# A new order of work at the entry and the segment turns of a feed-forward block

## The chip, the cores and the metric

The kernel runs on one core of one Trainium2 chip: TensorE (matmuls), VectorE, ScalarE, GpSimd and SyncE (DMA queues), each with its own instruction stream, tied together by semaphores. The metric is device time in microseconds (us), lower is better.

## The reference

One layer of a hybrid encoder over two sequences (1024 and 512 tokens of 1024 features, with 16 meta tokens in front): a norm, one input projection, two kinds of windowed attention, a norm for each, an output projection, and then the feed-forward part, which is where the change lies:

```
mix = jnp.concatenate([_rmsnorm(oa, outn_a_g), _rmsnorm(ob, outn_b_g)], axis=-1)
x = x + mix @ w_out
h = _rmsnorm(x, norm2_g)
x = x + (jax.nn.silu(h @ w_gate) * (h @ w_up)) @ w_down
```

The hidden width is 2816; all values are 32-bit floats.

## The kernel before

Products are made in near 32-bit precision from three matmuls: each operand is split in a high and a low part, and `product()` (L396 to L398) adds high x high, low x high and high x low. ScalarE writes high parts (`sth`, `mvh`, `acth`, `dh`), VectorE and GpSimd subtract them to get low parts (`stl`, `mvl`, `actl`, `dl`).

The feed-forward part goes over three segments of 512 tokens. Each segment has 11 cycles (`PASS`), one for 256 hidden columns; `cycles` (L690) writes the first two and the last of a segment out (q = 0, 1, 10) and loops over the rest (q is None). The 33 cycles c run through without a gap. In a cycle TensorE makes the gate of its columns, then the up part, then `down` of the cycle before, 8 blocks of 6 matmuls (a tile of 128 tokens t, half of the 1024 columns each). Gate and up are 2 x 2 block products in a scheme of seven products in place of eight, 12 matmuls each: seven standing operands (weights or sums of them: `weight_sums`, four a matrix, L1992 to L1998) against seven moving ones (tokens or sums of them: `token_sum`, L2013, eight instructions a segment). Products are combined by VectorE: `first_sums` (`u`, L2024, L2027) make room in PSUM for products 6 and 7, `last_sum` (L2033) gives the result. ScalarE makes silu, VectorE multiplies (`times`, L2043), splits (`act_low`, L2047), and adds what `down` gives to y (`add_down`, L2055). `down` waits before its third block, and at each later one, for an add two blocks ago.

The moving parts of the next segment are made in the last cycle of a segment, the turn (c = 10 and 21): seven `mvh` on ScalarE, seven `mvl` on VectorE (L2017). The entry is cycle 0 with what leads to it: the last output projection tiles are added to y (`mix_adds`, L1963), normed (`normed2`, `xn`, L1941), transposed by TensorE (`turn2`, L2417) and copied out by ScalarE (`mix_out`, `qm`, L1536), while the gate of segment 0 begins. Tiles (5,0) and (5,1) are the last two, and belong to segment 2.

Nothing plans the order: the order of the code is the order of each engine's queue, and an engine stands still at the first instruction that waits. GpSimd makes `stl` 0, 3, 4, 5 and 6 (L1195) and the two `dl` (L1201); VectorE makes `stl` 1 and 2 (L2002). SyncE loads the weights of `down` (`draw`) once `turn2` is through. Some buffers share memory: `xn[0]` with the end of `stl`, `xn[1]` with the first `draw`, `junk2` with the first `dl`.

Of the kernel before, what the change touches and what calls it, by code (L numbers as in the profile page):

```python
# [12 lines left out]
P = 128  # L13
# [51 lines left out]
def hybrid_encoder_layer(nc, x_prompt, x_sample, meta_tokens, t5_table, norm1_g, w_in, qn_a_g, kn_a_g,  # L65
# [134 lines left out]
    g2 = s("g2", [P, D])  # L200
    junk2 = s("junk2", [P, D])
    osq = s("osq", [P, KT, P])
    osum = [s(f"osum{i}", [P, 2, P]) for i in range(2)]
# [27 lines left out]

    tsum = [[at(f"tsum0{i}", [P, 4, 2 * P], F32, a) for i, a in enumerate((dl1_at, t_at, t_at + 4096, t_at + 8192))]]
    tsum += [[at(f"tsum1{i}", [P, 4, 2 * P], F32, qm_at[0] + i * 4096) for i in range(4)]] * 2
# [10 lines left out]
    with ExitStack() as ctx:  # L244
# [806 lines left out]
        def _(pool):  # L1051
# [160 lines left out]
            for i in ST_POOL:  # L1212
                if i == 5:
                    pool.wait_ge(turned2, 22)
                standing_low(0, graw, i)
# [5 lines left out]
        def _(act):  # L1221
# [349 lines left out]

            def standing_high(n, raw, i):
                if i in S_NEEDED:
                    act.wait_ge(s_done, n * 4 + S_NEEDED[i])
                wait(act, prod, n * 7 + i - 6)
                act.activation(sth[:, i, :, :], standing(raw, i), ACT.Copy).then_inc(st_hi, 1)  # L1576
# [35 lines left out]
            def ffn_cycle(c, g, q):  # L1612
                gate_n, up_n = c * 2, c * 2 + 1
                last = q == PASS - 1 and g == NSEG - 1

                def up_high(i):
                    standing_high(up_n, uraw, i)
# [12 lines left out]
                for i in range(3):  # L1630
                    up_high(i)
                wait(act, act_lo, c * 2)
                silu((0, 0), X, prod, gate_n * 7 + 4)
                for i in range(3, 7):
                    up_high(i)
                for i, at_ in enumerate(ORDER):
                    silu(at_, hidden(*at_), comb, gate_n * 5 + 3 + i)
                if last:
                    down_high(c)
                else:  # L1640
                    block21(c * 2 + 2, graw, gate_in, c + 1)
                first_product(up_n)
                for i in range(7):
                    gate_high(i)
                if q == 0 and g == 0:
                    mix_out(5, 1)

# [3 lines left out]
            act.wait_ge(mix_mm, 24)  # L1651
            for i in range(7):
                moving_high(0, i)
                standing_high(0, graw, i)
                if i == 0:
                    mix_out(4, 1)
                elif i == 2:
                    act.wait_ge(y_spilled[2], 32)
                    first_product(0)
                elif i == 3:  # L1660
                    block21(1, uraw, up_in, 0)
            mix_ss(5, 1)
            mix_out(5, 0)
            act.activation(ssq[:, 0:1], eps[:, :], ACT.Silu)
# [5 lines left out]
        def _(dve):  # L1670
# [261 lines left out]

            def normed2(i, slot, first):
# [5 lines left out]
                if not first:  # L1939
                    dve.wait_ge(turned2, tile_ * 2 - 2)  # L1940
                dve.scalar_tensor_tensor(out=xn[slot][:, :],  # L1941
                                         in0=y[:, bass.ds(tile_, 1), :].rearrange("p o c -> p (o c)"),
                                         scalar=r_, in1=g2[:, :], op0=ALU.mult, op1=ALU.mult).then_inc(xn2_done, 1)
# [43 lines left out]

            def weight_sums(n, raw):

                a = quarters(raw)  # L1990
                dve.wait_ge(a21_out, n + 1)
                dve.tensor_tensor(S1, A21_OR_S2, a[1, 1], ALU.add).then_inc(s_done, 1)  # L1992
                dve.tensor_tensor(a[1, 0], a[0, 0], A21_OR_S2, ALU.subtract).then_inc(s_done, 1)
                dve.wait_ge(s_done, n * 4 + 2)
                dve.tensor_tensor(A21_OR_S2, S1, a[0, 0], ALU.subtract).then_inc(s_done, 1)
                wait(dve, st_lo_pool, n * 5)
                dve.wait_ge(s_done, n * 4 + 3)
                dve.tensor_tensor(sum4[:, :, :], a[0, 1], A21_OR_S2, ALU.subtract).then_inc(s_done, 1)  # L1998

            def standing_low(n, raw, i):  # L2000
# [58 lines left out]
            def ffn_cycle(c, g, q):  # L2059
# [8 lines left out]

                if q == 0 and g == 1:
                    dve.wait_ge(turned2_out, 24)  # L2070

                def tokens_sum(n):
                    if q in (0, 1) and g < NSEG - 1 and n < 4:
                        token_sum(g + 1, 4 * q + n)

                tiles = down_tiles(g, q)
                if not first:
                    act_low(c - 1, 0)
                    act_low(c - 1, 1)
                weight_sums(up_n, uraw)  # L2080
                if not first:
                    first_sums(gate_n)
                standing_low(up_n, uraw, 1)
                standing_low(up_n, uraw, 2)
                for i in range(3):
                    last_sum(gate_n, i, hidden(*ORDER[i]))
                if first:
                    normed2(5, 1, False)
                    dve.wait_ge(turned2_out, 16)
                    for n in range(4):  # L2090
                        tokens_sum(n)
                else:
                    for t in tiles[0]:
                        add_down(c - 1, g, q, t, tokens_sum)
# [6 lines left out]
                if not last:  # L2101
                    standing_low(c * 2 + 2, graw, 2)
                times(c, up_n, -1)
                for i in range(3):
                    last_sum(up_n, i, (Y, Z, W)[i])
                    times(c, up_n, i)
                    if i < 2:
                        tokens_low(1 + i)
                tokens_low(3)
                if not first:  # L2110
                    for t in tiles[1]:
                        add_down(c - 1, g, q, t, tokens_sum)
                        if t < 3:
                            tokens_low(4 + t)

            group_sums(5, 0)
            group_inverses(5, 0)
            for half in range(2):
# [4 lines left out]
            dve.wait_ge(turned2_out, 8)  # L2123
            dve.wait_ge(y_spilled[1], 32)
            for n in range(4):
                token_sum(0, n)
            group_inverses(5, 1)
            mix_adds(5, 1, 0)
            weight_sums(0, graw)
            normed2(5, 0, False)  # L2130
            token_sum(0, 4)
            token_sum(0, 5)
            mix_adds(5, 1, 1)
            moving_low(0, 0)
            standing_low(0, graw, 1)
            moving_low(0, 1)
            standing_low(0, graw, 2)
            moving_low(0, 2)
            dve.wait_ge(y_spilled[2], 32)
            token_sum(0, 6)  # L2140
            token_sum(0, 7)
            moving_low(0, 3)
            first_sums(0)
            for i in range(4, 7):
                moving_low(0, i)
# [8 lines left out]
        def _(pe):  # L2154
# [253 lines left out]

            def turn2(i, slot, first=False):

                pe.wait_ge(xn2_done, i * 2 + slot + 1)
                for b in range(2):
                    if not first:
                        pe.wait_ge(turned2_out, i * 4 + slot * 2 + b - 1)
                    for k in range(4):
                        c = (4 * b + k) * P
                        op = pe.transpose(bank[4 + b][:, k * P:(k + 1) * P], xn[slot][:, c:c + P], ident[:, :])  # L2417
                    op.then_inc(turned2, 1)
# [9 lines left out]
            def seven_products(n, c, g, q, gate):  # L2428
                for i in range(7):
                    if i == 0 and gate and q == 0 and g == 0:  # L2430
                        pe.wait_ge(mix_add, 24)
                    if i == 2 and gate and q == 0 and g == 0:
                        turn2(5, 0)
                    if gate and q == 0:
# [34 lines left out]
            def ffn_cycle(c, g, q):  # L2469
# [75 lines left out]
```

## Time and profile before

| | us |
|---|---|
| median of 3 runs | 1969.75 |
| lowest, highest | 1966.92, 1971.46 |
| profiled execution | 1972.3 |
| its span | 1970.5 |
| TensorE busy | 1860.9 (94%) |
| VectorE busy | 1301.2 (66%) |
| ScalarE busy | 1003.8 (51%) |
| GpSimd busy | 959.2 (49%) |

The span is the time from the first to the last instruction; what is missing to the execution's own time (1.8 us) lies around it. TensorE's mean granted clock is 0.977. Over the whole kernel TensorE stands first on the chain that ended last (56%), VectorE follows with 5%. The feed-forward part begins at about 900 us.

### The profile page before, as it was taken

How to read it: one execution, taken by the hardware profiler on the slowest of the kernel's cores; microseconds unless marked ns; L12 is line 12 of the kernel's file. 1: busy time of each engine (PE TensorE's matmuls, PEld its weight loads, DVE VectorE, ACT ScalarE, POOL GpSimd, SP SyncE). 2: the span in 40 equal slices, each digit the busy share in tenths (PEclk: the TensorE clock that was granted, in tenths of full speed). 3: DMA queues.
4: the chain of work that ended last, by engine and by line, in shares of the span. 5: the costliest groups of instructions: out<-in, count | busy, mean ns of one | idle time of the engine just before them, and what ended most of it. 6: DMA issues, size and time to landing. Idle time of an engine off the chain costs nothing.

```text
span 1970.5 us, 35333 instructions
## 1 busy us (share of the span) xinstructions
PE 1860.9 (94%) x12047; PEld 1670.4 (85%) x12047; DVE 1301.2 (66%) x2345; ACT 1003.8 (51%) x2085; POOL 959.2 (49%) x811
## 2 busy tenths in 40 slices
PE   5998898999898989997999999999999999999998
PEld 4797677999677877886899999899999989999997
DVE  2656657888566876548666666776666676666664
ACT  3555456888535883345444354544444354444432
POOL 1334235765335651114556464646556464645543
PEclk7999998999998998999999999999999999999999
DMA  5443632454322435011332332343332335323221
GB/s 155 131 144 113 169 98 72 112 150 135 97 86 84 148 114 202 32 63 56 120 116 86 105 106 85 108 171 108 103 109 89 103 101 178 107 86 123 89 85 65
DMA packets 184323, 217.10 MB, mean 110 GB/s; under 512 B 13124, under 2 KB 162100, under 8 KB 183964
## 3 DMA queue, kind: packets, MB, share of 16 engines
q1 hardware_dynamic: 184220, 215.77, 34.9%
q8 instruction: 60, 0.98, 0.2%
q14 instruction: 43, 0.35, 0.1%
HBM read 197.34 MB, written 27.27 MB: 114 GB/s over the span
## 4 chain that ended last, share of the span: by engine, by line
PE 56%; DVE 5%; ACT 2%; issue 2%; POOL 1%; DMA 0%; ACTq 0%; POOLq 0%; DVEq 0%; SPq 0%
PE bank L396 19%; PE bank L397 18%; PE bank L398 18%; DVE mvl L2017 1%; POOL msl L1124 1%; ACT msh L1501 0%; DVE qm L1914 0%; ACT logit L1407 0%; DVE tsum L2013 0%; ACT qm L1431 0%; DVE pmeta L1854 0%; DVE logit L1839 0%; PE bank L2305 0%; DVE ptl L1846 0%; PE bank L2283 0%
## 5 line engine op out<-in xcount | busy, mean ns | idle before, releaser
L396 PE MATMUL bank<-mvh,sth 128*128 128x256 f32 x1848 | 526.4, 285 | 17.6 <-DVE act_f L2033 5.6
L398 PE MATMUL bank<-mvh,stl 128*128 128x256 f32 x1848 | 525.3, 284 | 0.0
L397 PE MATMUL bank<-mvl,sth 128*128 128x256 f32 x1848 | 525.3, 284 | 0.0
L396 PEld LDWEIGHTS bank<-mvh,sth 128*128 128x128 f32 x1848 | 356.8, 193 | 20.9 <-issue 16.9
L397 PEld LDWEIGHTS bank<-mvl,sth 128*128 128x128 f32 x1848 | 357.0, 193 | 1.2
L398 PEld LDWEIGHTS bank<-mvh,stl 128*128 128x128 f32 x1848 | 356.9, 193 | 0.0
L1201 POOL TENSOR_TENSOR dl<-draw,dh 128x1024 fp32r<-128x1024 f32 x66 | 157.9, 2414 | 365.9 <-ACT dh L1594 365.9
L2055 DVE TENSOR_TENSOR y<-bank,y 128x512 f32<-128x512 f32 x264 | 182.4, 691 | 163.9 <-PE bank L398 163.0
L1056 POOL TENSOR_TENSOR wl<-wraw,wh 128x1024 fp32r<-128x1024 f32 x54 | 130.5, 2418 | 263.5 <-ACT wh L1252 263.5
L1195 POOL TENSOR_TENSOR stl<-graw,sth 128x512 fp32r<-128x512 f32 x132 | 178.2, 1350 | 101.6 <-ACT sth L1576 97.4
L396 PE MATMUL bank<-dh,acth 128*128 128x512 f32 x528 | 209.5, 397 | 7.7 <-DVE y L2055 5.3
L396 PE MATMUL bank<-hth,wh 128*128 128x512 f32 (+2 forms) x512 | 198.1, 387 | 12.1 <-DVE htl L1764 8.6
L397 PE MATMUL bank<-dl,acth 128*128 128x512 f32 x528 | 208.4, 395 | 0.0
L398 PE MATMUL bank<-dh,actl 128*128 128x512 f32 x528 | 207.9, 394 | 0.0
L1610 ACT ACTIVATE acth<-act_f 128x512 fp32r<-128x512 f32 x66 | 38.2, 624 | 322.3 <-PE bank L398 314.3
L398 PE MATMUL bank<-hth,wl 128*128 128x512 f32 (+2 forms) x512 | 187.5, 366 | 0.0
L397 PE MATMUL bank<-htl,wh 128*128 128x512 f32 (+2 forms) x512 | 186.6, 364 | 0.0
L1195 POOL TENSOR_TENSOR stl<-uraw,sth 128x512 fp32r<-128x512 f32 x132 | 169.6, 1309 | 4.6 <-ACT sth L1576 4.6
L1730 DVE RECIPROCAL rt_p<-rt_p 128x512 f32<-128x512 f32 (+2 forms) x30 | 84.4, 2826 | 79.0 <-ACT rt_p L1321 79.0
L1407 ACT ACTIVATE logit<-logit,negm 128x274 f32<-128x274 f32 (+1 forms) x192 | 113.8, 593 | 38.9 <-DVE negm L1839 37.8
L396 PEld LDWEIGHTS bank<-hth,wh 128*128 128x128 f32 x512 | 98.3, 192 | 38.1 <-POOL wl L1056 12.9
L396 PEld LDWEIGHTS bank<-dh,acth 128*128 128x128 f32 x528 | 99.7, 189 | 30.9 <-DVE y L2055 6.5
(248 smaller groups left out, 4257.6 us busy)
## 6 DMA issues: line engine op xcount, KB each, us to landing
graw<-in_w_gate SPq DMA_DIRECT2D x33, 1024.0 KB, 5.4
uraw<-in_w_up SPq DMA_DIRECT2D x33, 1024.0 KB, 5.4
draw<-in_w_down SPq DMA_DIRECT2D x66, 512.0 KB, 4.1
wraw<-in_w_in SPq DMA_DIRECT2D x54, 512.0 KB, 3.9
bias_rows<-table_a SPq DMA_DIRECT2D x36, 192.0 KB, 3.1
out<-y SPq DMA_DIRECT2D x12, 512.0 KB, 3.0
bias<-table_b SPq DMA_DIRECT2D x28, 201.0 KB, 2.6
table_a<-line_a_dram SPq DMA_DIRECT2D x8, 576.0 KB
```

Source lines behind the costliest of these rows:

```text
L396: pe.matmul(out, lhs[0], rhs[0], start=start, stop=False, skip_group_check=True)
L397: pe.matmul(out, lhs[0], rhs[1], start=False, stop=False, skip_group_check=True)
L398: return pe.matmul(out, lhs[1], rhs[0], start=False, stop=stop, skip_group_check=True)
L1056: pool.tensor_tensor(wl[G % 2][:, :, :], wraw[G % 2][:, :, :], f32(wh[G % 2][:, :, :]), ALU.subtract).then_inc(w_lo, 1)
L1124: pool.tensor_tensor(msl[slot][:, :, :], mix_tile(i, slot), f32(msh[slot][:, :, :]), ALU.subtract).then_inc(ms_lo, 1)
L1195: pool.tensor_tensor(stl[:, i, :, :], standing(raw, i), f32(sth[:, i, :, :]), ALU.subtract).then_inc(st_lo_pool, 1)
L1201: pool.tensor_tensor(dl[j][:, :], draw[j][:, :], f32(dh[j][:, :]), ALU.subtract).then_inc(down_lo, 1)
L1407: act.activation(x, x, ACT.Exp, bias=negm[:, h % 2, t:t + 1], scale=-1.0, accum_out=lsum[:, h % 2, t:t + 1]).then_inc(expd, 1)
L1610: act.activation(acth[:, j, :], act_f[:, j, :], ACT.Copy).then_inc(act_hi, 1)
L1730: op = dve.reciprocal(rt[:, u0:u0 + w], rt[:, u0:u0 + w])
L2017: dve.tensor_tensor(mvl[:, i, :, :], moving(g, i), f32(mvh[:, i, :, :]), ALU.subtract).then_inc(mv_lo, 1)
L2055: dve.tensor_tensor(yt, DOWN_BANK[half][:, :], yt, ALU.add).then_inc(y_add, 1)
```

## The change

The arithmetic is the same; instructions change places, and two buffers. On VectorE at the turn, `mvl` 2 to 6 of the next segment go behind the pairs of adds of `down`. At the entry, `xn` of tiles (5,0) and (5,1) go to the end of cycle 0 and get buffers of their own (`last_xn`); the first `mvl` goes ahead of the last `mix_adds`; three of the four weight sums of the first up matrix go between `mvl` 4 and 5 and the fourth behind the last sums of the gate. Token sums of the next segment are all made in the segment's second cycle instead of four in the first and four in the second; those of segment 0 go earlier. TensorE makes `turn2(5,0)` before the last up product of cycle 0 instead of before the third gate product. ScalarE's silu and copies of those tiles follow. GpSimd's and SyncE's orders don't change.

```diff
-    tsum = [... (dl1_at, t_at, t_at + 4096, t_at + 8192) ...]
+    last_xn = [xn[1], junk2]
+    tsum = [... (t_at, t_at + 4096, dl1_at, t_at + 8192) ...]
...
             for i in ST_POOL:
                 if i == 5:
-                    pool.wait_ge(turned2, 22)
+                    pool.wait_ge(turned2, 18)
...
+                if q == 0 and g == 0:
+                    up_high(0)
+                    silu((0, 0), X, prod, gate_n * 7 + 4)
+                    up_high(1)
+                    up_high(2)
...
                 for i in range(7):
                     gate_high(i)
-                if q == 0 and g == 0:
-                    mix_out(5, 1)
+                    if q == 0 and g == 0 and i >= 5:
+                        mix_out(5, i - 5)
...
             for i in range(7):
+                if i == 0:
+                    standing_high(0, graw, 0)
+                    moving_high(0, 0)
+                    mix_out(4, 1)
+                    continue
                 moving_high(0, i)
                 standing_high(0, graw, i)
...
+                elif i == 4:
+                    mix_ss(5, 1)
-            mix_ss(5, 1)
-            mix_out(5, 0)
...
+            def fourth_sum(n, raw):
+                a = quarters(raw)
                 wait(dve, st_lo_pool, n * 5)
                 dve.wait_ge(s_done, n * 4 + 3)
                 dve.tensor_tensor(sum4[:, :, :], a[0, 1], A21_OR_S2, ALU.subtract).then_inc(s_done, 1)
...
                 def tokens_sum(n):
-                    if q in (0, 1) and g < NSEG - 1 and n < 4:
-                        token_sum(g + 1, 4 * q + n)
+                    if q == 1 and g < NSEG - 1:
+                        token_sum(g + 1, n)
...
-                weight_sums(up_n, uraw)
                 if not first:
+                    weight_sums(up_n, uraw)
                     first_sums(gate_n)
                 standing_low(up_n, uraw, 1)
-                standing_low(up_n, uraw, 2)
+                if not first:
+                    standing_low(up_n, uraw, 2)
                 for i in range(3):
                     last_sum(gate_n, i, hidden(*ORDER[i]))
+                    if first and i == 1:
+                        standing_low(up_n, uraw, 2)
                 if first:
-                    normed2(5, 1, False)
-                    dve.wait_ge(turned2_out, 16)
-                    for n in range(4):
-                        tokens_sum(n)
+                    fourth_sum(up_n, uraw)
...
+                if first:
+                    for slot in range(2):
+                        normed2(5, slot, False, True)
                 times(c, up_n, -1)
                 for i in range(3):
                     last_sum(up_n, i, (Y, Z, W)[i])
                     times(c, up_n, i)
-                    if i < 2:
-                        tokens_low(1 + i)
-                tokens_low(3)
+                    if i == 0:
+                        tokens_low(1)
                 if not first:
                     for t in tiles[1]:
                         add_down(c - 1, g, q, t, tokens_sum)
-                        if t < 3:
-                            tokens_low(4 + t)
+                        tokens_low(2 + t)
+                    if turn:
+                        tokens_low(6)
...
             weight_sums(0, graw)
-            normed2(5, 0, False)
-            token_sum(0, 4)
-            token_sum(0, 5)
+            moving_low(0, 0)
             mix_adds(5, 1, 1)
-            moving_low(0, 0)
...
             moving_low(0, 2)
+            moving_low(0, 3)
             dve.wait_ge(y_spilled[2], 32)
             token_sum(0, 6)
             token_sum(0, 7)
-            moving_low(0, 3)
             first_sums(0)
-            for i in range(4, 7):
+            moving_low(0, 4)
+            bank_sums(1, uraw)
+            for i in range(5, 7):
                 moving_low(0, i)
...
                 for i in range(7):
-                    if i == 0 and gate and q == 0 and g == 0:
-                        pe.wait_ge(mix_add, 24)
-                    if i == 2 and gate and q == 0 and g == 0:
-                        turn2(5, 0)
+                    if i in (0, 2) and gate and q == 0 and g == 0:
+                        pe.wait_ge(mix_add, 23 + i // 2)
+                    if i == 6 and not gate and q == 0 and g == 0:
+                        turn2(5, 0, last=True)
...
                 if first:
-                    turn2(5, 1)
+                    turn2(5, 1, last=True)
                     pe.wait_ge(turned2_out, 24)
```

VectorE at the entry before, from the second `u` of gate 0 (it ends in PSUM as `u_156`; `uraw` is the up weights, `sum_149` the fourth weight sum):

```order
L2027 TENSOR_TENSOR u_156<-bank,u_155 128x256 [waits comb,prod]
L2017 TENSOR_TENSOR mvl<-tsum_161,mvh 128x1024 [waits mv_hi]
L2017 TENSOR_TENSOR mvl<-qm,mvh 128x1024 [waits mv_hi]
L2017 TENSOR_TENSOR mvl<-tsum_162,mvh 128x1024 [waits mv_hi]
L1992 TENSOR_TENSOR bank<-bank,uraw 128x512 [waits a21_out]
L1993 TENSOR_TENSOR uraw<-uraw,bank 128x4x128
L1995 TENSOR_TENSOR bank<-bank,uraw 128x512 [waits s_done]
L1998 TENSOR_TENSOR sum_149<-uraw,bank 128x512 [waits s_done,st_lo_pool]
L2002 TENSOR_TENSOR stl<-bank,sth 128x512 [waits st_hi] x2
L2033 TENSOR_TENSOR act_f<-bank,u_156 128x256 [waits comb,prod] x2
```

The same place after:

```order
L2047 TENSOR_TENSOR u_156<-bank,u_155 128x256 [waits comb,prod]
L2037 TENSOR_TENSOR mvl<-tsum_161,mvh 128x1024 [waits mv_hi]
L2004 TENSOR_TENSOR bank<-bank,uraw 128x512 [waits a21_out]
L2005 TENSOR_TENSOR uraw<-uraw,bank 128x4x128
L2007 TENSOR_TENSOR bank<-bank,uraw 128x512 [waits s_done]
L2037 TENSOR_TENSOR mvl<-qm,mvh 128x1024 [waits mv_hi]
L2037 TENSOR_TENSOR mvl<-tsum_162,mvh 128x1024 [waits mv_hi]
L2022 TENSOR_TENSOR stl<-bank,sth 128x512 [waits st_hi]
L2053 TENSOR_TENSOR act_f<-bank,u_156 128x256 [waits comb,prod] x2
L2022 TENSOR_TENSOR stl<-bank,sth 128x512 [waits st_hi]
L2053 TENSOR_TENSOR act_f<-bank,u_155 128x256 [waits comb,prod]
L2014 TENSOR_TENSOR sum_149<-uraw,bank 128x512 [waits s_done,st_lo_pool]
```

Three of the weight sums stand between two `mvl` now, one `stl` and the fourth sum behind last sums (`act_f`), and `xn` is gone from here.

VectorE at the first turn before, from the fourth `mvl` on (`tsum_16x` and `qm` are the next segment's tokens and their sums, `y` the adds of `down`):

```order
L2017 TENSOR_TENSOR mvl<-qm,mvh 128x1024 [waits mv_hi]
L2055 TENSOR_TENSOR y<-bank,y 128x512 [waits down_mm] x2
L2017 TENSOR_TENSOR mvl<-tsum_165,mvh 128x1024 [waits mv_hi]
L2055 TENSOR_TENSOR y<-bank,y 128x512 [waits down_mm] x2
L2017 TENSOR_TENSOR mvl<-qm,mvh 128x1024 [waits mv_hi]
L2055 TENSOR_TENSOR y<-bank,y 128x512 [waits down_mm] x2
L2017 TENSOR_TENSOR mvl<-tsum_166,mvh 128x1024 [waits mv_hi]
L2055 TENSOR_TENSOR y<-bank,y 128x512 [waits down_mm] x2
L2047 TENSOR_TENSOR actl<-act_f,acth 128x512 [waits act_hi,turned2_out]
L2047 TENSOR_TENSOR actl<-act_f,acth 128x512 [waits act_hi]
```

The same place after, from the first add on:

```order
L2075 TENSOR_TENSOR y<-bank,y 128x512 [waits down_mm] x2
L2037 TENSOR_TENSOR mvl<-tsum_163,mvh 128x1024 [waits mv_hi]
L2075 TENSOR_TENSOR y<-bank,y 128x512 [waits down_mm] x2
L2037 TENSOR_TENSOR mvl<-qm,mvh 128x1024 [waits mv_hi]
L2075 TENSOR_TENSOR y<-bank,y 128x512 [waits down_mm] x2
L2037 TENSOR_TENSOR mvl<-tsum_165,mvh 128x1024 [waits mv_hi]
L2075 TENSOR_TENSOR y<-bank,y 128x512 [waits down_mm] x2
L2037 TENSOR_TENSOR mvl<-qm,mvh 128x1024 [waits mv_hi]
L2037 TENSOR_TENSOR mvl<-tsum_166,mvh 128x1024 [waits mv_hi]
L2067 TENSOR_TENSOR actl<-act_f,acth 128x512 [waits act_hi] x2
```

An `mvl` stands behind each pair of adds, two behind the last, and then the two `actl`.

## Rows read from the trace of the kernel before

**Rows 1.** Windows; busy us of each engine, granted PE clock, DMA share, GB/s.

```profile
900.00:950.00 50.00, 35.68 (x240) 34.37 (x241) 38.43 (x54) 29.31 (x53) 27.86 (x17) 0.87 0.30 95
1000.00:1200.00 200.00, 200.00 (x1375) 186.07 (x1375) 130.24 (x231) 88.06 (x165) 108.79 (x74) 1.00 0.30 98
```

**Rows 2.** Timeline, ScalarE's `acth`, one pair a cycle; start, us, what, idle before.

```profile
1225.25 1.15 ACT L1610 ACTIVATE acth<-act_f 128x512 fp32r<-128x512 f32 x2 [10.01 <-PE bank L398]
...
1261.26 1.15 ACT L1610 ACTIVATE acth<-act_f 128x512 fp32r<-128x512 f32 x2 [11.69 <-PE bank L398]
...
1292.54 1.15 ACT L1610 ACTIVATE acth<-act_f 128x512 fp32r<-128x512 f32 x2 [10.01 <-PE bank L398]
...
1574.06 1.15 ACT L1610 ACTIVATE acth<-act_f 128x512 fp32r<-128x512 f32 x2 [10.01 <-PE bank L398]
...
1608.77 1.16 ACT L1610 ACTIVATE acth<-act_f 128x512 fp32r<-128x512 f32 x2 [10.39 <-PE bank L398]
```

**Rows 3.** Timeline, TensorE, down blocks in both turns.

```profile
1245.72 0.39 PE L396 MATMUL bank<-dh,acth 128*128 128x512 f32 x1
...
1251.31 0.80 PE L396 MATMUL bank<-dh,acth 128*128 128x512 f32 x1 [2.66 <-DVE y L2055]
...
1254.04 0.46 PE L396 MATMUL bank<-dh,acth 128*128 128x512 f32 x1
...
1258.27 0.40 PE L396 MATMUL bank<-dh,acth 128*128 128x512 f32 x1
...
1600.10 0.50 PE L396 MATMUL bank<-dh,acth 128*128 128x512 f32 x1 [2.64 <-DVE y L2055]
```

**Rows 4.** Timeline, VectorE, first turn.

```profile
1250.58 1.27 DVE L2055 TENSOR_TENSOR y<-bank,y 128x512 f32<-128x512 f32 x2
...
1262.00 1.29 DVE L2047 TENSOR_TENSOR actl<-act_f,acth 128x512 fp32r<-128x512 f32 x2
...
1266.45 0.42 DVE L2027 TENSOR_TENSOR u<-bank,u 128x256 f32<-128x256 f32 x1
```

**Rows 5.** Timeline, TensorE, entry of the feed-forward part.

```profile
901.45 0.35 PE L396 MATMUL bank<-mvh,sth 128*128 128x256 f32 x1 [4.15 <-DVE mvl L2017]
...
920.26 0.55 PE L396 MATMUL bank<-mvh,sth 128*128 128x256 f32 x1 [5.63 <-DVE act_f L2033]
...
933.72 0.55 PE L396 MATMUL bank<-mvh,sth 128*128 128x256 f32 x1 [3.36 <-DVE u L2027]
...
939.84 0.39 PE L396 MATMUL bank<-mvh,sth 128*128 128x256 f32 x1 [0.82 <-ACT qm L1536]
```

**Rows 6.** Timeline, GpSimd, after the first turn.

```profile
1263.44 4.78 POOL L1201 TENSOR_TENSOR dl<-draw,dh 128x1024 fp32r<-128x1024 f32 x2 [11.66 <-ACT dh L1594]
```

**Rows 7.** Timeline, VectorE, entry, beside GpSimd's `stl`.

```profile
905.94 1.22 DVE L2017 TENSOR_TENSOR mvl<-qm,mvh 128x1024 fp32r<-128x1024 f32 x1
...
910.58 2.31 DVE L2017 TENSOR_TENSOR mvl<-qm,mvh 128x1024 fp32r<-128x1024 f32 x1
...
924.93 3.48 DVE L2013 TENSOR_TENSOR tsum<-qm 128x512 f32<-128x512 f32 x2
```

**Rows 8.** Timeline, GpSimd, the same stretch.

```profile
905.45 2.86 POOL L1195 TENSOR_TENSOR stl<-graw,sth 128x512 fp32r<-128x512 f32 x1 [5.55 <-ACT sth L1576]
...
911.76 2.27 POOL L1195 TENSOR_TENSOR stl<-graw,sth 128x512 fp32r<-128x512 f32 x1
...
926.14 1.73 POOL L1195 TENSOR_TENSOR stl<-graw,sth 128x512 fp32r<-128x512 f32 x1
```

**Rows 9.** Timeline, VectorE, a steady cycle.

```profile
982.29 0.42 DVE L2033 TENSOR_TENSOR act_f<-bank,u 128x256 f32<-128x256 f32 x1 [0.55 <-PE bank L398]
```

**Rows 10.** Timeline, VectorE, entry, before `mvl` and before the last sums.

```profile
897.48 1.29 DVE L2013 TENSOR_TENSOR tsum<-qm 128x512 f32<-128x512 f32 x2
...
918.50 1.29 DVE L2002 TENSOR_TENSOR stl<-bank,sth 128x512 fp32r<-128x512 f32 x2 [0.67 <-ACT sth L1576]
```

**Rows 11.** Timeline, ScalarE, entry.

```profile
896.46 1.06 ACT L1582 ACTIVATE mvh<-qm 128x1024 fp32r<-128x1024 f32 x1 [3.29 <-PE bank L398]
```

More of the change, by code:

```diff
@@ L229, in hybrid_encoder_layer @@
     assert BASE + s.offset <= END
-    tsum = [[at(f"tsum0{i}", [P, 4, 2 * P], F32, a) for i, a in enumerate((dl1_at, t_at, t_at + 4096, t_at + 8192))]]
+    tsum = [[at(f"tsum0{i}", [P, 4, 2 * P], F32, a) for i, a in enumerate((t_at, t_at + 4096, dl1_at, t_at + 8192))]]
     tsum += [[at(f"tsum1{i}", [P, 4, 2 * P], F32, qm_at[0] + i * 4096) for i in range(4)]] * 2
@@ L1569, in _, with standing_high @@
             group_root(5, 1)
-            def standing_high(n, raw, i):
+            def standing_high(n, raw, i, after_banks=False):
                 if i in S_NEEDED:
-                    act.wait_ge(s_done, n * 4 + S_NEEDED[i])
+                    act.wait_ge(s_done, n * 4 + (3 if after_banks else S_NEEDED[i]))
                 wait(act, prod, n * 7 + i - 6)
@@ L1616, in up_high @@
                 def up_high(i):
-                    standing_high(up_n, uraw, i)
+                    standing_high(up_n, uraw, i, q == 0 and g == 0 and i == 1)
                 def gate_high(i):
@@ L1629, in ffn_cycle @@
                     first_product(gate_n)
[L1630 to L1633, printed above, removed]
+                if q == 0 and g == 0:
[3 more added lines that the diff above has]
+                    up_high(2)
+                else:
+                    for i in range(3):
+                        up_high(i)
+                    wait(act, act_lo, c * 2)
+                    silu((0, 0), X, prod, gate_n * 7 + 4)
                 for i in range(3, 7):
@@ L1652, in _ @@
             for i in range(7):
+                if i == 0:
[3 more added lines that the diff above has]
+                    continue
                 moving_high(0, i)
                 standing_high(0, graw, i)
[L1655 to L1657 removed]
+                if i == 2:
                     act.wait_ge(y_spilled[2], 32)
@@ L1931, in _, with normed2 @@
                                          in1=f32(woh[:, k, :]), op0=ALU.mult, op1=ALU.subtract).then_inc(wo_lo, 1)
-            def normed2(i, slot, first):
+            def normed2(i, slot, first, last=False):
                 tile_ = i * 2 + slot
@@ L1938, in normed2 @@
                 dve.wait_ge(y_inv, tile_ + 1)
-                if not first:
+                if last:
+                    dve.wait_ge(turned2, 20)
+                elif not first:
                     dve.wait_ge(turned2, tile_ * 2 - 2)
-                dve.scalar_tensor_tensor(out=xn[slot][:, :],
+                dve.scalar_tensor_tensor(out=(last_xn if last else xn)[slot][:, :],
                                          in0=y[:, bass.ds(tile_, 1), :].rearrange("p o c -> p (o c)"),
@@ L1985, in _, with bank_sums @@
                 mixed(i, i - 1)
-            def weight_sums(n, raw):
+            def bank_sums(n, raw):
                 a = quarters(raw)
@@ L1998, in weight_sums @@
                 dve.tensor_tensor(sum4[:, :, :], a[0, 1], A21_OR_S2, ALU.subtract).then_inc(s_done, 1)
+            def weight_sums(n, raw):
+                bank_sums(n, raw)
+                fourth_sum(n, raw)
             def standing_low(n, raw, i):
@@ L2067, in tokens_low @@
                         moving_low(g + 1, i)
-                if q == 0 and g == 1:
-                    dve.wait_ge(turned2_out, 24)
+                if q == 1 and g < 2:
+                    dve.wait_ge(turned2_out, 16 + 8 * g)
                 def tokens_sum(n):
-                    if q in (0, 1) and g < NSEG - 1 and n < 4:
-                        token_sum(g + 1, 4 * q + n)
+                    if q == 1 and g < NSEG - 1:
+                        token_sum(g + 1, n)
                 tiles = down_tiles(g, q)
@@ L2112, in ffn_cycle @@
                         add_down(c - 1, g, q, t, tokens_sum)
-                        if t < 3:
-                            tokens_low(4 + t)
+                        tokens_low(2 + t)
+                    if turn:
+                        tokens_low(6)
             group_sums(5, 0)
             group_inverses(5, 0)
+            dve.wait_ge(turned2_out, 8)
+            dve.wait_ge(y_spilled[1], 32)
+            for n in range(4):
+                token_sum(0, n)
             for half in range(2):
@@ L2122, in _ @@
             normed2(4, 1, False)
[L2123 to L2126, printed above, removed]
+            token_sum(0, 4)
+            token_sum(0, 5)
             group_inverses(5, 1)
@@ L2407, in mix, with turn2 @@
                                 turn2(4, 0)
-            def turn2(i, slot, first=False):
+            def turn2(i, slot, first=False, last=False):
                 pe.wait_ge(xn2_done, i * 2 + slot + 1)
@@ L2416, in turn2 @@
                         c = (4 * b + k) * P
-                        op = pe.transpose(bank[4 + b][:, k * P:(k + 1) * P], xn[slot][:, c:c + P], ident[:, :])
+                        op = pe.transpose(bank[4 + b][:, k * P:(k + 1) * P], (last_xn if last else xn)[slot][:, c:c + P], ident[:, :])
                     op.then_inc(turned2, 1)
```

## The prediction

> **What bounds the kernel now.** I read the window table first. Inside the feed-forward part TensorE is the limit without a break: over 1000 to 1200 us it is busy for 200.00 of 200.00 us at a granted clock of 1.00, while VectorE has 130.24 us of work and GpSimd 108.79 [rows 1]. So nothing that is taken from VectorE in a steady cycle can show. Over 900 to 950 us, where the feed-forward part begins, TensorE is busy for only 35.68 of 50.00 us, at a mean clock of 0.87, so for a part of it at the lower of its two levels [rows 1]. ScalarE's activation `acth` at L1610 starts once in every cycle, so its starts measure the cycles: 1261.26 to 1292.54 is 31.28 us, a steady one; 1225.25 to 1261.26 is 36.01, the first turn, 4.73 us too long; 1574.06 to 1608.77 is 34.71, the second turn, 3.43 us too long [rows 2]. The change thus has three places to work on: the entry (14 us of TensorE's idle time at most) and two turns (8.2 us in all).
>
> At the first turn TensorE's rows say what is lost. The third down block (a half tile of `down`, 6 matmuls) waits 2.66 us for VectorE's add at L2055; then its six matmuls take 1251.31 to 1254.04 = 2.73 us, where a block at full clock takes 1.39 (the next three, 1254.04 to 1258.27, take 4.23 with one slow first matmul). 2.66 + 1.34 = 4.0 us [rows 3]. At the second turn the same wait is 2.64 us, and only the first matmul is slow, +0.11: 2.75 us [rows 3]. The add is late because VectorE has put three `mvl` groups (the low parts of the next segment's tokens) in front of it: it starts at 1250.58, though its product was ready long before [rows 4].
>
> At the entry the idle time has four heads: 4.15 us on the first `mvl` (901.45), 5.63 on `act_f`, the last sum of the gate (920.26), 3.36 on `u`, the first sum of the gate of cycle 1 (933.72), 0.82 on ScalarE's copy of the last transposed tile (939.84) [rows 5]. After 920.26 and 933.72 the first matmul has 0.55 us, a low clock again.
>
> **The change part by part: the turns.** Edit one moves `mvl` 2 to 6 behind the add pairs. The first add then follows `times`, about 1248.0, before the third block is due (1245.72 + 2 x 1.39 = 1248.5). Each later pair of adds is followed by one `mvl`: 1.27 + 1.13 (an `mvl` of 1.22 us less the 0.09 by which VectorE's rows overlap) against 2.78 for two blocks, so the adds keep up; I leave 0.25 us for the pair that meets GpSimd's last `stl`. `down` ends at 1245.72 + 8 x 1.39 + 0.25 = 1257.1 = T' instead of 1261.06: **-3.95 us**. The second turn likewise, with its 2.75 us: **-2.7 us**.
>
> But the edit puts `mvl` 5 and 6 behind the last add, where before the two `actl` (L2047) followed at once. Before, `actl` ran at 1262.00 to 1263.29, and GpSimd's two `dl`, 4.78 us together, began at 1263.44, when `actl` had just ended: they did not meet [rows 4, 6]. Now the last add ends at T'+0.8, `mvl` 5 and 6 at T'+3.07; `dl` asks at 1263.44 less 1261.06 = T'+2.38, 0.7 us before VectorE's next instruction can start. The rows show what then happens: such an instruction (both inputs in SBUF: `mvl`, `tsum`, `actl`) and one of GpSimd's exclude each other for their whole length. `mvl` at 910.58 takes 2.31 us instead of 1.22, the `stl` at 911.76 takes 2.27 and not 1.27; at 924.93 two `tsum` of 0.6 us take 3.48, since an `stl` that came at 926.14, 0.5 us ahead of the second `tsum`, went first [rows 7, 8]. An alternating pair of `mvl` and `stl` needs about 2.2 us (2.27 and 2.31 less their overlap), so VectorE loses 1.1 to an `stl` of 1.27, that is its length less 0.17; to a `dl` (2.39) it loses 2.2. So: T'+3.07, `dl` 2.2, `actl` 0.6, `dl` 2.2, `actl` 0.6: T'+8.65. From there to the end of `u` it is 1266.87 less 1263.29, about 3.5 us [rows 4]: T'+12.15. The sixth gate product needs `u` and is due at T' + 5 x 1.44 = T'+7.2. **TensorE waits 4.9 us at each turn**, where it did not wait before. A TensorE that has stood still for 2.66 to 5.63 us has shown from one slow matmul (+0.11) to a slow product's worth (+1.3) behind it [rows 3, 5]; I take the middle, **+0.65**. Turn 1: -3.95 + 4.9 + 0.65 = +1.6; turn 2: -2.7 + 4.9 + 0.65 = +2.85.
>
> Here the Trainium skill ("SBUF — State Buffer", "Who interferes with whom") has a rule: whoever issues first gets the shared ports for the whole instruction, and the other is blocked altogether. By it `dl` wins both times, the 4.9 us above. The trace agrees at 911.76 and 926.14, but not at 905.45: there GpSimd's `stl` came 0.49 us before the `mvl` at 905.94, took 2.86 us, and the `mvl` its usual 1.22 [rows 7, 8]; by that row the second `dl` would lose, and the wait be 2.75 us.
>
> Edit two puts all 8 token sums of the next segment into a segment's second cycle, where 4 were: 4 x 0.6 = 2.4 us more of VectorE, which has over 10 us free in a cycle [rows 1]. What counts is the last one, 0.6 us in front of `actl`; later in that chain VectorE waits 0.55 us for TensorE (982.29) [rows 9]. At most 0.1 us: nothing.
>
> **The entry.** I laid the row durations end to end in the new order. (a) The first `mvl` no longer stands behind `xn`, two `tsum` and two adds (897.48 and on), but it needs ScalarE's first `mvh`, which took 1.06 us from 896.46 and now also stands behind an `sth` of half its size [rows 10, 11]: 899.3, so the gate starts at 899.6, not 901.45. (b) Little of it lasts: `mvl` 3 moves ahead of two `tsum`, and the three bank sums (2.0 us) go in front of `mvl` 5; product 5 starts at 911.1, product 6 at 914.9, later than in the order before. (c) Then comes the gain: the first last-sum no longer waits for the fourth weight sum and both `stl` (0.67 idle and 1.29 at 918.50) [rows 10]; product 7 starts at about 917.2 instead of 920.26. (d) The 3.36 us on `u` go too: `xn` of the last tile and four `tsum` (3.48 us for the first two alone, at 924.93) leave the way of the weight sums [rows 7]. (e) What comes in their place: both `xn` now follow `u` and two `stl`, each about 2.1 us since GpSimd's `stl` alternate with them. So `turn2(5,0)`, now in front of the last up product, waits about 2 us, and that product 2 us more for the next sum. Gate 1 starts at 935.7, where the same walk of the order before, without any low clock, has 937.5 (the trace has 939.84): **-1.9 us**. SyncE's transfer of `draw` still follows the last transpose and moves with it; POOL's and SP's orders stay.
>
> Low clock cost 939.84 - 937.54 = 2.3 us before. With none of it after, the entry gains 4.1; with twice as much it gains nothing and loses 0.5. I keep it as it was, since there are as many stalls (five) as before.
>
> **Sum.** -1.9 + 1.6 + 2.85 = +2.55 us. The profiled execution took 1972.3 us (span 1970.5), 2.55 above the median of 1969.75 of the runs shown; the change is put on the median: **1972.3 us**.
>
> **Rivals.** *R1, one loss per turn.* The second `dl`, only some 0.5 us ahead of the second `actl`, loses, as at 905.45: the wait is 2.75. Turns -0.55 and +0.7, entry -1.9: 1968.0. Against it stands 926.14, the same lead with the same length of instruction. *R2, the turns pay.* VectorE keeps both `actl` in front, because it issues back to back: `u` is ready at T'+7.75, the wait is 0.55, without a clock loss. -3.4 - 2.15 - 1.9 = -7.45: 1962.3. Against it stand all rows where GpSimd had waited 0.5 us or more; for it, that GpSimd waits for a semaphore here and VectorE does not. *R3, slower.* The wait of 4.9 us at the sixth gate product of both new segments brings a whole slow product each time (+1.3), and the low clock at the entry doubles: 2.25 + 3.5 + 0.5 = +6.25: 1976.0. It decides where TensorE's rows after `u` show twelve slow matmuls; for it speak 920.26 and 1251.31, against it 1600.10.
>
> **How the numbers follow.** Forecast 0.42, R1 0.20, R2 0.24, R3 0.14. A measurement of this kernel can tell about 0.2%, 3.9 us: 1965.85 and 1973.65 are the bounds. With some 2 us of spread about each case, faster is 0.03 + 0.05 + 0.20 + 0 = 0.28; within, 0.24 + 0.14 + 0.04 + 0.02 = 0.44; slower, 0.15 + 0.01 + 0 + 0.12 = 0.28. The range takes in R2 and R3 with part of their spread: 1961.0 to 1978.0; the forecast's own is 1970 to 1975.
>
> **What would show it.** Right: no wait on `y` at the third down block of a turn; `actl` as two instructions of about 2.8 us behind `mvl` 6, and the sixth gate product of the next segment waiting about 4.9 us for `u`; at the entry product 7 at about 917 and a wait for `xn` in front of the last up product. Cycles of 37 to 38 us would then stand where 36.01 and 34.71 stood, split over two: the turn short, the next one long. Wrong: two `actl` of 0.6 us in a row (R2), or one of 0.7 us after one of 2.8 (R1); or a gate 1 that starts after 940.

## The result, and the profile after

| | median us | runs | ratio to before, 95% interval |
|---|---|---|---|
| before | 1971.46 | 9 | |
| after | 1978.3 | 9 | 1.0034 [1.0025, 1.0043] |

The change makes the kernel slower by 0.34%, 6.7 us by the ratio (4.9 to 8.5). The forecast was +2.55 us on a median of 1969.75, too little to be told from noise, in a range from 1961.0 to 1978.0. The profiled execution took 1982.02 us, its span is 1980.2.

ScalarE's `acth` measures the cycles as in [rows 2]. In the kernel after:

```profile
1225.49 0.63 ACT L1611 ACTIVATE acth<-act_f 128x512 fp32r<-128x512 f32 x1 [10.01 <-PE bank L399]
...
1257.72 0.63 ACT L1611 ACTIVATE acth<-act_f 128x512 fp32r<-128x512 f32 x1 [7.91 <-PE bank L399]
...
1296.24 0.63 ACT L1611 ACTIVATE acth<-act_f 128x512 fp32r<-128x512 f32 x1 [10.01 <-PE bank L399]
...
1577.76 0.63 ACT L1611 ACTIVATE acth<-act_f 128x512 fp32r<-128x512 f32 x1 [10.01 <-PE bank L399]
...
1610.00 0.63 ACT L1611 ACTIVATE acth<-act_f 128x512 fp32r<-128x512 f32 x1 [7.92 <-PE bank L399]
...
1648.22 0.63 ACT L1611 ACTIVATE acth<-act_f 128x512 fp32r<-128x512 f32 x1 [10.01 <-PE bank L399]
```

The end of the second pair before, which [rows 2] leaves out:

```profile
1640.05 1.15 ACT L1610 ACTIVATE acth<-act_f 128x512 fp32r<-128x512 f32 x2 [10.01 <-PE bank L398]
```

The first turn takes 32.23 us (36.01 before) and the cycle behind it 38.52 (31.28). Together 70.75 against 67.29: +3.46. At the second, 32.24 + 38.22 = 70.46 against 34.71 + 31.28 = 65.99: +4.47. So the turns are 3.8 and 2.5 us shorter, close to the forecast, and the next cycle gives back 7.2 and 6.9. All other cycles from cycle 2 on are the same to 0.1 us in both kernels, the one in segment 1 with eight token sums among them (31.36 in both).

VectorE at the first turn after, in place of [rows 4]; start, length, what:

```profile
1258.33 1.22 DVE L2037 TENSOR_TENSOR mvl<-qm,mvh 128x1024 fp32r<-128x1024 f32 x1
...
1259.46 1.22 DVE L2037 TENSOR_TENSOR mvl<-tsum,mvh 128x1024 fp32r<-128x1024 f32 x1
...
1260.59 2.90 DVE L2067 TENSOR_TENSOR actl<-act_f,acth 128x512 fp32r<-128x512 f32 x1
...
1263.41 2.86 DVE L2067 TENSOR_TENSOR actl<-act_f,acth 128x512 fp32r<-128x512 f32 x1
...
1269.43 0.42 DVE L2047 TENSOR_TENSOR u<-bank,u 128x256 f32<-128x256 f32 x1
```

GpSimd there, in place of [rows 6]:

```profile
1259.90 3.04 POOL L1202 TENSOR_TENSOR dl<-draw,dh 128x1024 fp32r<-128x1024 f32 x1 [9.79 <-ACT dh L1595]
...
1262.90 2.82 POOL L1202 TENSOR_TENSOR dl<-draw,dh 128x1024 fp32r<-128x1024 f32 x1
```

TensorE, at the sixth gate product of the new segment and at the end of the low clock behind it, then the same wait at the second turn:

```profile
1270.00 0.55 PE L397 MATMUL bank<-mvh,sth 128*128 128x256 f32 x1 [5.14 <-DVE u L2047]
...
1273.98 0.41 PE L397 MATMUL bank<-mvh,sth 128*128 128x256 f32 x1
...
1274.36 0.28 PE L399 MATMUL bank<-mvh,stl 128*128 128x256 f32 x1
...
1622.29 0.55 PE L397 MATMUL bank<-mvh,sth 128*128 128x256 f32 x1 [5.14 <-DVE u L2047]
```

Two `mvl` are done, then the pair of `actl` takes 5.68 us where it took 1.29; `dl` asks at 1259.90 while the second `mvl` runs, and its pair takes 5.83 instead of 4.78. `u` ends at 1269.85, and TensorE has waited 5.14 us. Then it runs for 4.2 us at the lower of its two levels (a matmul has 0.41 us, 0.28 from 1274.36 on). The window table, with the columns of [rows 1], has a granted clock of 0.50 there:

```profile
1270.00:1274.00 4.00, 4.00 (x19) 4.00 (x20) 1.81 (x4) 2.06 (x5) 2.81 (x3) 0.50 0.00 0
```

At the entry the two traces must first be laid on one point, since the whole part ahead of it was 2.63 us later in the profiled execution after: the transposes of the last tile before the gate begin at 898.89, those of the kernel before at 896.26:

```profile
896.26 1.03 PE L2417 MATMUL bank<-ident,xn 128*128 128x128 f32 x8
```

TensorE after, in place of [rows 5]:

```profile
898.89 0.27 PE L2441 MATMUL bank<-ident,xn 128*128 128x128 f32 x1
...
902.25 0.55 PE L397 MATMUL bank<-mvh,sth 128*128 128x256 f32 x1 [2.32 <-DVE mvl L2037]
...
920.67 0.41 PE L397 MATMUL bank<-mvh,sth 128*128 128x256 f32 x1
...
930.68 0.36 PE L397 MATMUL bank<-mvh,sth 128*128 128x256 f32 x1 [0.30 <-DVE u L2047]
...
933.81 0.33 PE L2441 MATMUL bank<-ident,xn 128*128 128x128 f32 x1 [1.47 <-DVE xn L1953]
...
936.78 0.55 PE L397 MATMUL bank<-mvh,sth 128*128 128x256 f32 x1 [1.88 <-DVE bank L2053]
...
941.40 0.39 PE L397 MATMUL bank<-mvh,sth 128*128 128x256 f32 x1 [0.74 <-ACT qm L1537]
```

On the clock of before, less 2.63, product 7 begins at 918.0 (920.26 before, forecast 917.2). The wait for `u` is 0.30 instead of 3.36; new are 1.47 for `xn` ahead of the transposes of tile (5,0), and 1.88 for the sum behind them. Gate 1 starts at 938.8 (939.84 before, forecast 1.9 us earlier): 1.1 us earlier. The next `acth`, at the end of cycle 1, where the gate of cycle 2 begins, starts at 975.34 - 2.63 = 972.7, 2.4 us earlier than before. `acth` before and after:

```profile
975.10 1.15 ACT L1610 ACTIVATE acth<-act_f 128x512 fp32r<-128x512 f32 x2 [10.10 <-PE bank L398]
```

```profile
975.34 1.15 ACT L1611 ACTIVATE acth<-act_f 128x512 fp32r<-128x512 f32 x2 [10.10 <-PE bank L399]
```

The other 1.3 us of the 2.4 are the clock in cycle 1 and not the new order: behind a wait of about 2 us for ScalarE (1.88 before, 2.04 after) TensorE ran at a granted clock of 0.50 before and of 1.00 after. Window tables, before and after:

```profile
947.00:950.40 3.40, 3.40 (x18) 3.40 (x18) 1.48 (x3) 1.54 (x4) 3.40 (x3) 0.50 0.02 7
```

```profile
948.00:951.40 3.40, 3.39 (x28) 3.40 (x29) 2.33 (x5) 2.45 (x6) 3.40 (x2) 1.00 0.05 16
```

Six traces have the entry of the change (this one, and those of entry alone, of `dl` behind `actl`, of one `mvl` earlier, of the filled wait and of `mvl` 5 and 6 behind `u`). Counted from the same transposes, gate 1 starts 0.6 to 1.6 us earlier than before in them, and cycle 2 0.6 to 2.4.

### The profile page after: what moved, and what is told of

It reads as the page before. It is cut to its first block, busy times and chain, and to the rows that moved or that the text cites. A ratio compares the mean times of both kernels' runs of the same rounds, so it can differ in the third digit from the quotient of the medians.

```text
span 1980.2 us, 35333 instructions
## 1 busy us (share of the span) xinstructions
PE 1869.0 (94%) x12047; PEld 1677.4 (85%) x12047; DVE 1308.3 (66%) x2345; ACT 1004.1 (51%) x2085; POOL 958.6 (48%) x811
## 4 chain that ended last, share of the span: by engine, by line
PE 56%; DVE 4%; ACT 2%; issue 2%; POOL 2%; DMA 1%; ACTq 0%; SPq 0%; POOLq 0%; DVEq 0%
PE bank L397 18%; PE bank L398 18%; PE bank L399 18%; DVE mvl L2037 1%; POOL msl L1125 1%; DVE actl L2067 1%; ACT msh L1502 0%; ACT logit L1408 0%; PE bank L2329 0%; DVE qm L1924 0%; ACT qm L1432 0%; DVE stl L2022 0%; DVE y L2075 0%; POOL bias L1103 0%; DMA draw<-in_w_down 0%
## 5 line engine op out<-in xcount | busy, mean ns | idle before, releaser
L1577 ACT ACTIVATE sth<-bank 128x512 fp32r<-128x512 f32 x132 | 72.0, 596 | 106.3 <-DVE sum L2014 105.6
```

## The experiments

The theory: `mvl` 5 and 6 behind the last add bring `actl` and `dl` together, GpSimd goes first twice, `u` comes 5 us late, and the low clock behind that wait costs another 2 us; the entry gains. The rivals: the entry or the token sums lose, or two `mvl` alone are the price, or what follows the wait is late work and not the clock. The first four ran on one chip beside 26 runs of before (median 1971.18), the others beside 29 (1971.53).

**Entry alone.** The turn as it was:

```diff
-                    if i == 0:
-                        tokens_low(1)
+                    if i < 2:
+                        tokens_low(1 + i)
+                tokens_low(3)
                 if not first:
                     for t in tiles[1]:
                         add_down(c - 1, g, q, t, tokens_sum)
-                        tokens_low(2 + t)
-                    if turn:
-                        tokens_low(6)
+                        if t < 3:
+                            tokens_low(4 + t)
```

> The change with the turn's order of VectorE put back to what it was before. Theory (the entry gains 1 to 2.4 us, the whole loss lies in the two turns): 1 to 2.4 us faster than before; the start of the gate of cycle 2 comes 2.4 us earlier against the same point of the end of the output projection, and the turn cycles are 36 and 34.7 us again. Rival (the entry's new order costs too, and the loss before 900 us in the profile of the change is its doing): 2 us or more slower than before.

Median 1970.35, ratio 0.9993 [0.9984, 1.0003]. That is 1.4 us faster than before, between 3.2 faster and 0.6 slower. In its trace the `acth` at the start of cycle 2 comes 76.77 us after the transposes named above, against 78.84 before and 76.45 after: the entry gains 2.1 us there, 0.7 of it up to gate 1. The second turn happens to take 36.19 us in this trace and not 34.71, since all of the first waiting block falls to the low clock (granted 0.50 over 1597.80 to 1601.00), and that takes most of the gain back. The rival is out: the entry does not lose.

**Turn alone.** The diff above the other way round, on the kernel before.

> The kernel before with the turn's new order of VectorE alone. Theory: the two cycles of each turn take 3.5 and 4.4 us more than before, 7.9 us together; each sixth gate product waits 5.1 us for u. Rival (the loss needs the entry's or the token sums' new place): within 2 us of before.

Median 1980.66, ratio 1.0048 [1.0034, 1.0062]. Cycles 32.22 + 38.85 and 32.23 + 38.40: +3.78 and +4.64, 8.4 us together, and the two sixth products wait 5.14 and 5.15 us. The turns' order alone makes the loss.

**`dl` behind `actl`.** VectorE's order is that of the change; only GpSimd is held:

```diff
+                if q == 0 and g:
+                    pool.wait_ge(act_lo, c * 2)
                 if q != 0 or g:
                     down_low(c - 1)
```

> The change, and GpSimd waits in the first cycle of segments 1 and 2 until both actl are made before it starts on dl; VectorE's order is that of the change. Theory (dl, which came 0.7 us earlier, goes ahead of each actl): the two actl take 1.3 us again, u comes 4.4 us earlier, the wait of 5.1 us falls to 0.7 and the slow matmuls behind it go: about 6.5 us a turn less than the change, 13 in all, so some 6 us faster than before. Rival (two mvl in front of actl are the price, whoever holds the ports): the wait stays above 4 us, within 2 us of the change.

Median 1966.98, ratio 0.9975 [0.9966, 0.9985]: 4.9 us faster than before, where some 6 were expected. VectorE, GpSimd and TensorE at the first turn:

```profile
1256.20 1.22 DVE L2039 TENSOR_TENSOR mvl<-tsum,mvh 128x1024 fp32r<-128x1024 f32 x1
...
1257.34 0.69 DVE L2069 TENSOR_TENSOR actl<-act_f,acth 128x512 fp32r<-128x512 f32 x1
...
1261.79 0.42 DVE L2049 TENSOR_TENSOR u<-bank,u 128x256 f32<-128x256 f32 x1
```

```profile
1258.70 2.40 POOL L1202 TENSOR_TENSOR dl<-draw,dh 128x1024 fp32r<-128x1024 f32 x1 [11.85 <-DVE actl L2069]
```

```profile
1262.36 0.35 PE L397 MATMUL bank<-mvh,sth 128*128 128x256 f32 x1 [0.75 <-DVE u L2049]
```

The two `mvl` still stand in front of `actl`, but the pair takes 1.29 us, TensorE waits 0.75, and no slow matmul follows. The cycles are 32.20 + 32.35, 6.2 us less than in the change; at the second turn 5.9. So `dl` going ahead of `actl` is shown to be the cause, and the two `mvl` alone leave a wait of 0.75.

**One `mvl` earlier.** `mvl` 2 ahead of the adds, 3 to 6 behind the four pairs:

```diff
-                    if i == 0:
-                        tokens_low(1)
+                    if i < 2:
+                        tokens_low(1 + i)
...
-                        tokens_low(2 + t)
-                    if turn:
-                        tokens_low(6)
+                        tokens_low(3 + t)
```

> The change, with mvl 2 ahead of the adds and mvl 3 to 6 behind the four pairs of adds, so that one mvl and not two stands between the last add and actl. Theory: dl then comes only some 0.4 us ahead of the second actl or with the first, VectorE keeps both in front, u is there when the sixth gate product is due, and the third down block waits 0.8 us in place of 2.66: about 3 and 1.8 us less than before at the turns, with the entry about 7 us faster than before. If dl wins one turn of the ports: a wait of 1.7 us, some 3 us faster than before. Rival (any mvl behind the last add costs the same lock): as slow as the change.

Median 1969.63, ratio 0.9989 [0.9980, 0.9998].

```profile
1258.35 1.22 DVE L2037 TENSOR_TENSOR mvl<-tsum,mvh 128x1024 fp32r<-128x1024 f32 x1
...
1259.48 0.69 DVE L2067 TENSOR_TENSOR actl<-act_f,acth 128x512 fp32r<-128x512 f32 x1
```

```profile
1259.92 2.51 POOL L1202 TENSOR_TENSOR dl<-draw,dh 128x1024 fp32r<-128x1024 f32 x1 [9.94 <-ACT dh L1595]
```

```profile
1249.05 0.51 PE L397 MATMUL bank<-dh,acth 128*128 128x512 f32 x1 [1.24 <-DVE y L2075]
...
1266.72 0.36 PE L397 MATMUL bank<-mvh,sth 128*128 128x256 f32 x1 [1.82 <-DVE u L2047]
```

The `actl` pair takes 3.51 us: one `dl` went first, and not two. TensorE waits 1.82 us for `u` (1.7 was the figure for one lost turn) and 1.24 for the add at the third block; nothing behind either is slow. 33.33 + 33.43 at the first turn is 0.5 less than before, 33.32 + 33.43 at the second is 0.8 more. The whole is 2.2 us faster by the ratio; 3 were expected for one lost turn, and 7 for none, which I had held to be likelier. `dl` begins at 1259.92, some 0.16 us before the second `actl` is due (1259.48 + 0.6), and that lead was enough.

**Needless matmuls in the wait.** 36 matmuls of product 6's shape into a bank that is free then, before the wait for `u`:

```diff
+                    if gate and q == 0 and g and i == 5:
+                        pe.wait_ge(y_add, c * 8 - 8)
+                        for k in range(12):
+                            product(pe, bank[4][:, 0:2 * P], (sth[:, 5, k % 4, :], stl[:, 5, k % 4, :]),
+                                    (mvh[:, 5, k % 4, :], mvl[:, 5, k % 4, :]), k == 0, k == 11)
```

> The change, and while the sixth gate product of a new segment waits for u, TensorE makes 36 needless matmuls of that product's shape into a bank that nobody reads until down begins it anew (0.12 us each, 4.3 us); the output is the same. Theory (behind the wait of 5.14 us the low clock costs another 2.1 us a turn, the term that the prediction put at 0.65): the idle wait falls to about 0.8 us, u comes no earlier, and the matmuls behind it are at full clock: the second of the two cycles takes 36.5 us in place of 38.5, about 4 us less than the change in all. Rival (the 2.1 us are work that comes late, not the clock): the cycle stays above 38 us.

Median 1973.91, ratio 1.0012 [1.0003, 1.0021], 4.3 us less than the change by the two ratios. VectorE's `actl`, TensorE's first matmul that counts, the clock behind it, and `acth` at both ends of the cycle:

```profile
1258.88 2.90 DVE L2067 TENSOR_TENSOR actl<-act_f,acth 128x512 fp32r<-128x512 f32 x1
```

```profile
1268.22 0.39 PE L397 MATMUL bank<-mvh,sth 128*128 128x256 f32 x1 [0.75 <-DVE u L2047]
```

```profile
1268.20:1272.00 3.80, 3.78 (x30) 3.68 (x31) 2.34 (x5) 2.63 (x6) 2.71 (x3) 1.00 0.03 9
```

```profile
1256.00 1.16 ACT L1611 ACTIVATE acth<-act_f 128x512 fp32r<-128x512 f32 x2 [7.90 <-PE bank L399]
...
1292.75 1.15 ACT L1611 ACTIVATE acth<-act_f 128x512 fp32r<-128x512 f32 x2 [10.01 <-PE bank L399]
```

The idle wait is 0.75 us, `actl` is as late as in the change (5.70 us for the pair), the granted clock is 1.00, and the cycles behind the turns are 36.75 and 36.74 instead of 38.52 and 38.22. So the low clock cost 1.77 and 1.48 us. Some 0.3 of the 2.1 is not the clock: the same 0.3 stands behind the waits of the two runs above where no matmul is slow (32.35 less 31.28 less 0.75; 33.43 less 31.28 less 1.82).

**`mvl` 5 and 6 behind `u`.**

```diff
                     for t in tiles[1]:
                         add_down(c - 1, g, q, t, tokens_sum)
-                        tokens_low(2 + t)
-                    if turn:
-                        tokens_low(6)
+                        if t < 3:
+                            tokens_low(2 + t)
...
                     first_sums(gate_n)
+                    if q == 0:
+                        moving_low(g, 5)
+                        moving_low(g, 6)
```

> The change, with mvl 5 and 6 of the turn taken out from between the last add and actl and put behind u in the next cycle. Theory: actl then runs before dl asks, u is ready 1.7 us before the sixth gate product is due, but both mvl ask while dl holds the ports and alternate with GpSimd: products 6 and 7 wait about 1 us each; about 5 us a turn less than the change, some 4 us faster than before. Rival (mvl 5 starves behind both dl and the stl that follow): waits of 3 us or more, as slow as before.

Median 1970.75, ratio 0.9999 [0.9990, 1.0009]: the 4 us did not come.

```profile
1256.19 0.69 DVE L2067 TENSOR_TENSOR actl<-act_f,acth 128x512 fp32r<-128x512 f32 x1
...
1260.98 2.59 DVE L2037 TENSOR_TENSOR mvl<-qm,mvh 128x1024 fp32r<-128x1024 f32 x1
...
1263.50 2.30 DVE L2037 TENSOR_TENSOR mvl<-tsum,mvh 128x1024 fp32r<-128x1024 f32 x1
```

```profile
1263.63 0.39 PE L397 MATMUL bank<-mvh,sth 128*128 128x256 f32 x1 [0.95 <-DVE mvl L2037]
...
1267.48 0.36 PE L397 MATMUL bank<-mvh,sth 128*128 128x256 f32 x1 [2.15 <-DVE act_f L2053]
```

`actl` is quick again. The first wait is 0.95 us as expected, the second 2.15 and not 1, since `last_sum` stands behind both `mvl` and two `stl` in VectorE's queue, which I had left out. 32.22 + 36.35 and 32.21 + 34.87: at the first turn a low clock follows the second wait (granted 0.69 over 1267.50 to 1271.00), at the second none does (1.00 over 1617.50 to 1621.00).

**`xn` in the gap of the entry.** The rest is the change:

```diff
                 if first:
                     fourth_sum(up_n, uraw)
+                    normed2(5, 0, False, True)
...
                 if first:
-                    for slot in range(2):
-                        normed2(5, slot, False, True)
+                    normed2(5, 1, False, True)
```

> The change, with xn of tile (5,0) made right behind the fourth weight sum, where VectorE idles for 2.6 us at the entry, and not behind both stl. Theory (the entry's new waits of 1.47 us for xn and 1.88 us for the sum behind it are the price of the late xn): the wait for xn goes and the one behind it falls below 1 us; 2 to 3 us faster than the change at the entry, the turns as in the change. Rival (the low clock or the wait for draw takes it back): within 1 us of the change at the start of the gate of cycle 2.

Median 1975.42, ratio 1.0017 [1.0008, 1.0025], against 1.0034 of the change.

```profile
930.01 0.27 PE L2441 MATMUL bank<-ident,xn 128*128 128x128 f32 x1
...
932.40 0.35 PE L397 MATMUL bank<-mvh,sth 128*128 128x256 f32 x1 [1.35 <-DVE bank L2053]
...
935.75 0.39 PE L397 MATMUL bank<-mvh,sth 128*128 128x256 f32 x1 [0.82 <-ACT qm L1537]
```

The transposes no longer wait, the sum behind them is waited for 1.35 us (I had said below 1). Gate 1 starts 38.46 us after the transposes of the point above, 4.05 us earlier than in the change; the `acth` at the start of cycle 2 comes 73.83 us after them, 2.6 earlier. The rest went to the low clock in cycle 1, which this trace has and that of the change has not: the rival's mechanism, though not in its size.

**Both mends.** `dl` behind `actl`, and `xn` in the gap.

> Both mends together: dl behind actl in the first cycle of segments 1 and 2, and xn of tile (5,0) behind the fourth weight sum. Theory: their gains add, about 4.2 us of the first against before and 2 to 3 us of the second: some 6 to 7 us faster than before. Rival (the entry's gain is given back by the low clock): 4 us, as the first alone.

Median 1961.46, ratio 0.9954 [0.9941, 0.9967]: 9 us faster than before, more than the 6 to 7 expected. The trace has 73.85 us to the start of cycle 2 (-5.0 against before), and turns of 32.21 + 32.33 and 32.22 + 32.33 (-2.75 and -1.44): -9.2 us. Against the first mend alone the entry gives 3.1 us.

## Why the prediction was wrong

**The turn's shorter `down`: right.** The wait of the third block is gone. -3.95 and -2.7 were forecast, -3.78 and -2.47 came (36.01 to 32.23, 34.71 to 32.24).

**The order of the ports: right.** `dl` went ahead of both `actl`, in both turns, as the row at 926.14 had it; the row at 905.45, the ground of R1, did not decide. Forecast 4.9 us of wait for `u`, measured 5.14 twice; holding `dl` back took it to 0.75. The Trainium skill's rule ("SBUF — State Buffer", "Who interferes with whom") agrees with these runs: whichever asked first had its whole instruction, even with a lead of some 0.16 us where one `mvl` was made earlier. The row at 905.45 stands alone: of the eight times that GpSimd's row began first in the trace of before, it is the only one where GpSimd did not go first, and the other nine traces have none. Why that `stl` lost with a lead of 0.49 stays open.

**The low clock behind the wait: the step that failed, in its size.** "I take the middle, +0.65" a turn; 2.1 us (7.24 longer, less 5.14) and 1.8 (6.94 less 5.14) came with it, of which the filled wait shows 1.77 and 1.48 to be the clock. The ends of the bound, +0.11 and +1.3, came from waits of 2.64 to 5.63 us, and the upper was one product's worth, 12 matmuls; after 1270.00 there are 19 slow ones, and 16 at the second turn. A slow matmul follows the last by 0.21 us instead of 0.12, so 19 and 16 of them cost about 1.8 and 1.5. The trace of before had more than the bound took in: 16 slow matmuls behind 946.96, +1.5 us (the 0.50 over 947.00 to 950.40 above). R3's clause on the clock was nearer, and too small as well. Of the 3.5 us by which the turns missed (7.93 instead of 4.45) this is 2.6, the longer wait 0.5 and `down` 0.4.

**The entry: right in sign, too large at gate 1.** -1.9 was forecast for the start of gate 1, and 1.1 came (0.6 to 1.6 in the six traces). That cycle 2 starts 2.4 us earlier, near the forecast's size, is partly luck: 1.3 of it is the low clock that cycle 1 had before and not after. The new waits came about as forecast (1.47 and 1.88, "about 2" each), and the 3.36 went but for 0.30. The product at 933.72, which the prediction puts in the gate of cycle 1, is the sixth of the up part of cycle 0; gate 1 begins at 939.84. The sum does not change by it.

**Token sums: right.** The cycle of segment 1 with eight of them has 31.36 us, as before.

Summed with the measured parts: -2.4 + 3.46 + 4.47 = +5.5 us, within the interval of 4.9 to 8.5. The rest up to the profiled spans' +9.7 is 2.63 ahead of the entry and 1.53 behind the last `acth`. The change touches neither: over the ten traces the same transposes begin between 894.60 and 898.89 in no relation to the edits.

The range ended 8.25 us above 1969.75, the median of three runs; over nine runs before has 1971.46, and the change lies 6.84 above that. So part of what put it outside the range is the base, and the greater part of the forecast's own error is the clock's.

## What to carry to other kernels

A TensorE wait has two prices, its own length and the slow matmuls behind it; where the wait is about 5 us, count both, at the largest figure seen and not the middle. When an edit puts instructions between two that were back to back on VectorE, look at what GpSimd starts in that time: the instruction that slips behind GpSimd's pays GpSimd's whole length each time, and one wait on GpSimd, which had slack (it had idled 9.79 us before `dl`), was cheaper than any order of VectorE that was tried. A gain and its loss can stand in two neighbouring cycles, so compare pairs.

## What the runs showed of the hardware

The same order gives cycles that differ by 1.3 to 1.5 us from run to run and turn to turn, by whether the clock falls behind a wait: 34.71 and 36.19 us for the second turn of one and the same order, 36.35 and 34.87 for the cycles behind the two turns with `mvl` 5 and 6 behind `u`. In the trace of before the granted clock is 0.50 behind the wait of 2.66 us at the first turn (1251.30 to 1254.00) and 1.00 behind that of 2.64 at the second (1600.00 to 1602.00). So a gain of 1 to 2 us that one trace shows is to be checked for such a fall before it is put down to the order. And idle TensorE time can be worth filling: 4.3 us of matmuls whose result nobody reads made the change 1.8 and 1.5 us faster behind its two turns, with a granted clock of 1.00 instead of 0.50.
